# Window attention of a two-block transformer kernel: the constant of the hidden keys written by VectorE, two jobs moved to GpSimd, weights of a gate split earlier

## The reference, cut to what matters

```python
h = rmsnorm_2(x, norm_g)                     # 512 x 1024
q, k, v, za, u, vs, zs, gm = split(h @ w_in) # q 16 heads of 64; k, v 2 heads; za, u, vs, zs 1024 wide
# keys of the own chunk of 64 tokens and of the two chunks before it
s = einsum('bnqhgd,bnkhd->bhgnqk', qc, kb) * 64 ** -0.5
s = where(valid, s, -1e30)
m = maximum(max(s), sink)                    # one sink value for each head
p = exp(s - m)
o = (p / (sum(p) + exp(sink - m))) @ vb
a   = (o * silu(za)) @ w_att_out
sgo = (chunked_spatial_gating(...) * silu(zs)) @ w_sg_out
```

## Time and profile before

| | us |
|---|---|
| median of 3 runs | 1279.54 (1279.12 to 1280.45) |
| profiled execution, own time | 1279.79 |
| its span in the profile | 1278.0 |
| TensorE busy | 1261.3 (99%) |
| VectorE busy | 729.8 (57%) |
| ScalarE busy | 548.2 (43%) |
| GpSimd busy | 84.2 (7%) |
| window attention, from the first mask product to the last gating's input | 859.2 to 959.5 |

### The profile page before, as it was taken

The page is one execution under the profiler, slowest core; times in us unless marked ns, Lnnn a source line. Parts: engine busy times, 40 slices in busy tenths (PEclk is TensorE's granted clock), DMA queues, the critical chain, the costliest instruction groups (busy, mean ns, idle before and its releaser), DMA issues.

```text
span 1278.0 us, 15814 instructions
## 1 busy us (share of the span) xinstructions
PE 1261.3 (99%) x6114; PEld 1058.4 (83%) x6114; DVE 729.8 (57%) x1185; ACT 548.2 (43%) x953; POOL 84.2 (7%) x129
## 2 busy tenths in 40 slices
PE   9999999999999999999999999999999999999997
PEld 8878888888888888888888888878888888888886
DVE  6885677753635444444443349858985436436554
ACT  5456565642334434343322233338763343223233
POOL 0002250220000000000000000002220000000000
PEclk9999999999999999999999999999999999999999
DMA  6241323133532232333323323331104322323221
GB/s 199 68 116 53 83 75 91 51 85 96 181 99 77 89 107 90 99 98 115 99 83 100 115 66 116 99 99 34 50 19 157 118 84 87 102 96 99 84 98 66
DMA packets 106956, 119.54 MB, mean 94 GB/s; under 512 B 13895, under 2 KB 89741, under 8 KB 106893
## 3 DMA queue, kind: packets, MB, share of 16 engines
q1 hardware_dynamic: 106876, 118.67, 29.5%
q10 hardware_dynamic: 16, 0.00, 0.0%
HBM read 113.42 MB, written 2.10 MB: 90 GB/s over the span
## 4 chain that ended last, share of the span: by engine, by line
PE 90%; DVE 6%; ACT 3%; issue 1%; POOL 0%; ACTq 0%; DVEq 0%; POOLq 0%
PE ps_mm L2013 56%; PE ps_mm L2048 23%; PE ps_s L2191 1%; DVE w_lo L1216 1%; PE ps_o L2222 1%; PE ps_o L2440 1%; ACT w_hi L685 1%; PE ps_mm L2105 1%; PE ps_s L2244 1%; PE ps_t L2202 1%; PE ps_t L2427 1%; DVE w_lo L1225 1%; DVE small L1816 1%; PE ps_o L2271 1%; DVE pt_lo L1836 1%
## 5 line engine op out<-in xcount | busy, mean ns | idle before, releaser
L2013 PE MATMUL ps_mm<-act_hi,w_hi 128*128 128x512 f32 x944 | 372.4, 394 | 2.8 <-DVE w_lo L1216 2.8
L2013 PE MATMUL ps_mm<-act_hi,w_lo 128*128 128x512 f32 x944 | 369.9, 392 | 0.0
L2013 PE MATMUL ps_mm<-act_lo,w_hi 128*128 128x512 f32 x944 | 369.8, 392 | 0.0
L1216 DVE TENSOR_TENSOR w_lo<-stage,w_hi 128x2048 fp32r<-128x2048 f32 (+5 forms) x78 | 158.4, 2031 | 160.7 <-ACT w_hi L685 160.5
L2013 PEld LDWEIGHTS ps_mm<-act_hi,w_hi 128*128 128x128 f32 x944 | 177.4, 188 | 39.2 <-DVE w_lo L1216 4.5
L2013 PEld LDWEIGHTS ps_mm<-act_hi,w_lo 128*128 128x128 f32 x944 | 177.4, 188 | 35.5
L2013 PEld LDWEIGHTS ps_mm<-act_lo,w_hi 128*128 128x128 f32 x944 | 177.5, 188 | 34.7
L685 ACT ACTIVATE w_hi<-stage 128x2048 fp32r<-128x2048 f32 (+5 forms) x79 | 133.7, 1693 | 159.9 <-PE ps_mm L2048 112.7
L1622 DVE TENSOR_TENSOR w_lo<-stage,w_hi 128x2048 fp32r<-128x2048 f32 x23 | 52.7, 2292 | 56.3 <-ACT w_hi L965 56.2
L2048 PE MATMUL ps_mm<-w_hi,act_hi 128*128 128x512 f32 (+2 forms) x208 | 77.6, 373 | 0.6 <-DVE lat L1352 0.5
L2048 PE MATMUL ps_mm<-w_lo,act_hi 128*128 128x512 f32 (+2 forms) x208 | 77.1, 370 | 0.0
(11 more groups left out here) (401 smaller groups left out, 2031.9 us busy)
## 6 DMA issues: line engine op xcount, KB each, us to landing
stage<-in_w_in SPq DMA_DIRECT2D x43, 1024.0 KB, 5.3
stage<-in_w_ffn_gate SPq DMA_DIRECT2D x11, 1024.0 KB, 5.3
stage<-in_w_ffn_up SPq DMA_DIRECT2D x11, 1024.0 KB, 5.3
stage<-in_w_ffn_down SPq DMA_DIRECT2D x10, 1024.0 KB, 5.0
stage<-in_w_out SPq DMA_DIRECT2D x4, 1024.0 KB, 5.7
stage<-in_w_att_out SPq DMA_DIRECT2D x4, 1024.0 KB, 5.2
stage<-in_w_sg_out SPq DMA_DIRECT2D x4, 1024.0 KB, 5.5
stage<-in_w_o SPq DMA_DIRECT2D x4, 1024.0 KB, 5.1
```

The costliest lines, as they stand in the source:

```text
L1216: V.tensor_tensor(w_lo[:, s, 0:k * w], stage[:, s, 0:k * w], w_hi[:, s, 0:k * w].bitcast(F32), ALU.subtract).then_inc(w_lo_made, 1)
L2013: ins = T.matmul(ps_mm[:, 2 * bank_slot + m, :], wt[:, kk, m * P:(m + 1) * P], acts[ap][:, kk, :], start=(r == 0), stop=(r == per - 1), sk ...
```

## The change

1. The mask product of each of the 32 pieces goes. The first score product starts the bank, and VectorE writes -1e30 into the corners of `ps_s` by memset, ahead of the maximum: one memset of 64 partitions x 128 elements for pieces 0 to 7, two for the others, and the maximum waits for the last one.
2. GpSimd computes `dsink` (32 times, 128x2) and the gating of zs (8 times), the latter in two instructions of 128x512 with a wait between them, in place of one on VectorE.
3. In the za loop, ScalarE and VectorE split unit za+i+2 at index i (i below 3), ahead of the Silu and behind the two `normed`; the low parts of the keys and of v come later (v's at i = 1), and the row block of `res` comes behind the two `normed`.

```diff
@@ block.gpsimd
-            for q in range(WIN_PIECES):
-                j0, c = 0 if q // 8 else P, 2 * (q % 4)
-                pool.wait_ge(rden_made, q + 1)
-                G.tensor_scalar(prob2[:, q % 4, 256 + j0:512], ...).then_inc(win_p_ready, 1)
+            pool.wait_ge(sink_landed, 16)
+            for p in range(WIN_STEPS + 2):
+                if p < WIN_PIECES:
+                    h, c = window_head(p % 8, 0), 2 * (p % 4)
+                    j = 16 * (p // 8 % 2) + h
+                    pool.wait_ge(win_max_made, p + 1)
+                    G.tensor_tensor(dsink[:, c:c + 2], sinkb[:, h:h + 3:2], nm2[:, j:j + 3:2], ALU.add
+                                    ).then_inc(sink_diff, 1)
+                if 1 <= p <= WIN_PIECES:
+                    q = p - 1
+                    j0, c = 0 if q // 8 else P, 2 * (q % 4)
+                    pool.wait_ge(rden_made, q + 1)
+                    G.tensor_scalar(prob2[:, q % 4, 256 + j0:512], ...).then_inc(win_p_ready, 1)
+                for u, m in WIN_STREAM.banks.get(p - 1, ()):
+                    n = 2 * (u - U0["zs"]) + m
+                    pool.wait_ge(z_tanh, n + 1)
+                    linked_after(G.tensor_scalar(tmp[:, m, :], tmp[:, m, :], 1.0, None, ALU.add))
+                    G.tensor_tensor(gu[:, n, :], tmp[:, m, :], gu[:, n, :], ALU.mult).then_inc(z_gated, 1)
@@ block.scalar
-                if i:
-                    hi(u + 1)
+                if i < 3:
+                    hi(u + 2)
@@ block.vector, the za loop
             for i in range(4):
                 u = U0["za"] + i
-                if i:
-                    lo(u + 1)
-                else:
+                if i == 0:
                     dve.wait_ge(v_turned, 1)
                     ... v2_hi
-                    ... v2_lo, k_lo
-                V.scalar_tensor_tensor(out=res[:, i, :], ...).then_inc(x3_made, 1)
                 for m in range(2):
                     normed(gz[:, 2 * i + m, :], u, m)
+                if i < 3:
+                    lo(u + 2)
+                if i == 0:
+                    ... k_lo
+                if i == 1:
+                    ... v2_lo
+                V.scalar_tensor_tensor(out=res[:, i, :], ...).then_inc(x3_made, 1)
                 if i == 3:
                     dve.wait_ge(x3_made, TT)
@@ block.vector, the window loop
                     dve.wait_ge(win_s_full, p + 1)
+                    sc = ps_s[:, p % 2, :].rearrange("p (e n) -> p e n", e=2)
+                    outside = link(V.memset(sc[0:CHUNK, :, 2 * P - CHUNK:2 * P], NEG))
+                    if b:
+                        outside = link(V.memset(sc[CHUNK:P, :, 0:CHUNK], NEG))
+                    after(outside)
                     after(link(V.tensor_reduce(mx, ps_s[...], AX.X, ALU.max, negate=True)))
                     V.tensor_tensor(nm2[:, j:j + 3:2], mx, nsinkb[:, h:h + 3:2], ALU.min).then_inc(win_max_made, 1)
-                    dve.wait_ge(win_max_made, p + 1)
-                    V.tensor_tensor(dsink[:, c:c + 2], ...).then_inc(sink_diff, 1)
...
-                for u, m in WIN_STREAM.banks.get(p - 1, ()):
-                    z_bank(m, 2 * (u - U0["zs"]) + m)
@@ block.tensor, the window loop
-                    ends = slice(0, 4, 3) if b else slice(3, 4)
-                    T.matmul(ps_s[...][:, :, ends, :], ident_r[:, :], window_r[...][:, :, ends, :],
-                             start=True, stop=False, skip_group_check=True)
                     for e in range(2):
                         T.matmul(out, q_split[...], k_hi[...],
-                                 start=False, stop=False, skip_group_check=True)
+                                 start=True, stop=False)
                         ins = T.matmul(out, q_split[...], k_lo[...],
-                                       start=False, stop=(e == 1), skip_group_check=True)
+                                       start=False, stop=True)
```

More of the change, by code:

```diff
@@ L659, in _ @@
                         pool.wait_ge(diff_rstd_made, hd + 1)
-            for q in range(WIN_PIECES):
-                j0, c = 0 if q // 8 else P, 2 * (q % 4)
-                pool.wait_ge(rden_made, q + 1)
-                G.tensor_scalar(prob2[:, q % 4, 256 + j0:512], prob2[:, q % 4, 256 + j0:512], rden2[:, c + 1:c + 2],
-                                None, ALU.mult).then_inc(win_p_ready, 1)
+            pool.wait_ge(sink_landed, 16)
[10 more added lines that the diff above has]
+                    pool.wait_ge(rden_made, q + 1)
+                    G.tensor_scalar(prob2[:, q % 4, 256 + j0:512], prob2[:, q % 4, 256 + j0:512], rden2[:, c + 1:c + 2],
+                                    None, ALU.mult).then_inc(win_p_ready, 1)
+                for u, m in WIN_STREAM.banks.get(p - 1, ()):
[3 more added lines that the diff above has]
+                    G.tensor_tensor(gu[:, n, :], tmp[:, m, :], gu[:, n, :], ALU.mult).then_inc(z_gated, 1)
         @block.scalar
@@ L1750, in _, with turned_values @@
             normed(kv[:, 0, :], u, 1)
[L1752 to L1756, removed]
+            def turned_values():
+                return ps_t[:, :].rearrange("p (t g n) -> p t g n", t=TT, g=AG)
+            halves = (slice(0, AD), slice(AD, 2 * AD))
             for i in range(4):
                 u = U0["za"] + i
-                if i:
-                    lo(u + 1)
-                else:
+                if i == 0:
                     dve.wait_ge(v_turned, 1)
[L1765 to L1771, removed]
+                    for half in halves:
+                        V.tensor_copy(v2_hi[:, :, :, half], turned_values()).then_inc(v2_wg_made, 1)
+                for m in range(2):
+                    normed(gz[:, 2 * i + m, :], u, m)
+                if i < 3:
+                    lo(u + 2)
+                if i == 0:
                     for g in range(AG):
@@ L1777, in _ @@
                                             ).then_inc(k_lo_made, 1)
+                if i == 1:
+                    for n, half in enumerate(halves):
+                        dve.wait_ge(v2_wg_made, n + 1)
+                        V.tensor_tensor(v2_lo[:, :, :, half], turned_values(), v2_hi[:, :, :, half].bitcast(F32),
+                                        ALU.subtract).then_inc(v2_wg_made, 1)
                 V.scalar_tensor_tensor(out=res[:, i, :], in0=res[:, i, :], scalar=rstd[:, i:i + 1], in1=gf_b[:, :],
                                        op0=ALU.mult, op1=ALU.mult).then_inc(x3_made, 1)
-                for m in range(2):
-                    normed(gz[:, 2 * i + m, :], u, m)
                 if i == 3:
@@ L1819, in _ @@
                     V.tensor_tensor(nm2[:, j:j + 3:2], mx, nsinkb[:, h:h + 3:2], ALU.min).then_inc(win_max_made, 1)
-                    c = 2 * (p % 4)
-                    dve.wait_ge(win_max_made, p + 1)
-                    V.tensor_tensor(dsink[:, c:c + 2], sinkb[:, h:h + 3:2], nm2[:, j:j + 3:2], ALU.add
-                                    ).then_inc(sink_diff, 1)
                 if 1 <= p <= NP:
@@ L2400, in _ @@
                     k0 = (b - 1) * P if b else 0
-                    ends = slice(0, 4, 3) if b else slice(3, 4)
-                    T.matmul(ps_s[:, p % 2, :].rearrange("p (e c n) -> p e c n", e=2, c=4)[:, :, ends, :],
-                             ident_r[:, :], window_r[:, :, :].rearrange("p e (c n) -> p e c n", c=4)[:, :, ends, :],
-                             start=True, stop=False, skip_group_check=True)
                     for e in range(2):
```

## The result

The changed kernel takes 1287.7 us (median of 4 runs, 1286.0 to 1288.0) against 1279.65 us before: ratio 1.0061, 95% interval 1.0048 to 1.0073. It is 8.1 us slower. I had forecast 1281.5 us, in a range from 1276.0 to 1287.0: the direction was right, the size was a quarter of the measured one, and the time lies 0.7 us outside the range. The profiled execution took 1287.59 us, its span is 1285.8 us, 7.8 us more than before.

The account below looks back on a forecast made before the run. TensorE was taken as busy 99% of the span, with VectorE near its limit in the attention. Terms +0.6 (VectorE), +1.6 and +0.3 (GpSimd), -0.5 (za) gave +2.0 us: 1281.5 us, range 1276.0 to 1287.0.

Parts of the forecast that it names:

- The 3.4 us of TensorE: Mask product in the window attention: removing it takes 3.4 us off TensorE, the most this can give.
- the za part: Za loop: the 1.7 us wait goes, 1.2 us is given back at the attention's door, so -0.5 us.
- the stretches with their reserve: Attention, by stretch: VectorE's additions are absorbed up to reserves of 0.6, 1.6 and 1.4 us; sum +0.6 us.
- both inside the reserve: Stretch 898.4 to 916.5: VectorE +0.6, TensorE -0.7, reserve 1.6, so -0.5 us with 0.2 left for uneven steps.
- Part 2: VectorE in an attention step: dsink and gatings leave, memsets come, +0.30 us in 24 steps; by stretches +0.6 us.
- Part 3: GpSimd in the attention: gatings make dsink late, 1.6 us, and shared SBUF reads cost VectorE 0.3 us.
- The memset's term: VectorE's memsets of 64x128 ahead of the maximum: 0.22 us each, 0.50 for two with waits, bounds 0.16 and 0.29 each.
- GpSimd's term: Six gatings on GpSimd: 1.6 us for late dsink (bounds 0.5 and 3.1), 0.3 for SBUF meetings (0 and 1.2).
- The rival's price: Attention: GpSimd stops VectorE's two-operand SBUF instructions until it ends, 6.5 us more, 1288 us; chance 0.12.
- TensorE waiting at the transposes for VectorE's low part, over 2 us in all: Expected sign in the attention's changed profile that VectorE's reserve is gone: over 2 us of such TensorE waits.
- Dear memsets: VectorE's attention steps: memsets cost 0.29 us each, +5.4 us in all, 1284.9 us; chance 0.08.
- TensorE stays the bound: Attention: two memsets cost under about 0.25 us, the 3.4 us come through, 1275.6 us; chance 0.18.

Follow-up runs that it names:

- run 4: The changed kernel with the gating of zs back on VectorE, dsink still on GpSimd: 1285.2 us, ratio 1.0045.
- run 1: The kernel before with only the new za loop (weights split sooner, row block of res behind the two normed): 1278.9 us, ratio 0.9995.
- run 3: The kernel before with only dsink and the gating of zs moved to GpSimd: 1279.6 us, ratio 1.0001.
- run 11: The kernel before with the new za loop, but the last row block of res ahead of the normed: 1277.9 us, ratio 0.9985.
- run 6: The changed kernel without the memsets, so without the mask: 1278.3 us, ratio 0.9991.
- run 8: The changed kernel with GpSimd's gating in four instructions of 256 columns in place of two of 512: 1286.1 us, ratio 1.0052.
- run 5: The changed kernel with dsink back on VectorE, the gating of zs still on GpSimd: 1290.1 us, ratio 1.0085.
- run 7: The changed kernel with the second memset on the first 64 partitions, so a wrong corner is masked: 1283.3 us, ratio 1.0031.
- run 9: The changed kernel with the two corner memsets in turned order in odd pieces, all corners masked: 1285.6 us, ratio 1.0049.
- run 10: The changed kernel with the last row block of res ahead of the two normed of unit za+3: 1285.6 us.

## Why the prediction was right or wrong

- **"VectorE is near its limit, what leaves TensorE is worth something only as far as VectorE follows"** held. The 3.4 us of TensorE bought next to nothing: without the memsets the kernel gains 1.2 us, of which the za part alone gives 0.7, with them it loses 8.1.
- **The step that failed: the stretches with their reserve.** I let VectorE's additions be absorbed up to a reserve, took the gatings' slots off on top, and so came to "both inside the reserve" and a gain for TensorE's two stretches. Beside the forecast of Part 2 and the lateness of Part 3 stands what the maxima say, from the first piece of a line to the last (us; run 4 has no gating on GpSimd):

| pieces | Part 2 | Part 3 | changed kernel | run 4 |
|---|---|---|---|---|
| 0 to 8 | -0.3 | 0.2 | +1.5, with 0.75 of clock | +0.7 |
| 8 to 15 | +0.7 | 1.0 | +2.0 | +1.75 |
| 15 to 21 | -0.5 | 0.3 | +1.8 | +0.9 |
| 21 to 23 | +0.6 | 0 | +1.3 | +1.3 |
| 23 to 30 | -0.3 | 0.45 | +0.9 | +1.0 |
| 30 to 31 | +0.4 | 0 | +0.55 | +0.4 |

The forecast missed most from 15 to 21, by 2.0 us, the first of TensorE's stretches, where both stops fall, and from 8 to 15 by 0.3 only.

- **The size of the two terms.** Without the gatings' slots my Part 2 is 0.4 + 1.5 + 0.2 + 0.6 + 0.7 + 0.4 = +3.8 us; run 4 against run 1, which differ in the mask and `dsink` alone, is +6.2. The gating's place was then worth 0.6 - 3.8 + 1.6 + 0.3 = -1.3 us to me; it measured +1.2 over pieces 10 to 31. Both terms were 2.5 us too low. The remaining 1.4 us of run 4's distance to the changed kernel, the scatter at the first maximum and the clock, were in no term.
- **The memset's term** was mis-sized. I took 0.22 us for the instruction and 0.50 for two with their waits; the row is 0.165, but with the pauses at the change of partitions the pair puts the maximum 0.52 us later behind the gating (0.09 + 0.46 - 0.03) and 0.63 behind other instructions (0.09 + 0.46 + the 0.08 of overlap lost). With 0.20 for `dsink` that is about +0.37 a step in place of +0.30. Run 4's loss from piece 10 to 31 is 5.3 us, and 21 x 0.37 is 7.8; that the 2.5 between them are VectorE's reserve is what is left over, not a measurement. The 0.03 of a result's wait I had counted, the held start I hadn't.
- **GpSimd's term:** 1.6 + 0.3 us forecast, 5.0 gross against 3.9 won. ScalarE waited 1.59, 0.43, 0.97 and 0.44 us where I had 1.7, 1.0, 1.3 and 0.95; the two of 0.4 did not show. The lateness was rather too high, and still the loss was larger, because I let ScalarE's pauses and the longer steps swallow most of it, and because the stops of VectorE that I gave 0.12 as a rival came true in two of six gatings, 1.06 us each, beside a third of 0.15. The Trainium skill, "SBUF — State Buffer", section "Who interferes with whom", says that a VectorE instruction with two SBUF inputs contends with a GpSimd one that reads SBUF, over ports that it calls an exclusive lock; its words "for the whole instruction", which I took for this case, stand there beside VectorE's two-port modes. The row at 905.68 agrees: stopped until GpSimd's product ends. In run 3 a minimum that began 0.21 us into the product took 1.10 us, up to its end as well. But a minimum at 876.88, begun 0.32 us into GpSimd's 1.50 us of adding 1, was over after 0.31 us, so here only the product with two inputs stopped VectorE to its end. The rows that made me doubt it were of GpSimd's scaling, which has one. The other four gatings cost no such stop, since no minimum or sum began during their products. The rival's price (6.5 us more) was too high for that reason. The last gating, which I had at no cost, did stop the full weight split at 971.20 (3.27 us in place of 2.29), but the kernel is 7.7 us behind at the maximum of piece 31 and 7.8 at its end.
- **The za part** was right: -0.5 forecast, -0.7 in run 1, with 1.0 us given back at the door by the medians (run 1 against run 11; 0.3 by their profiled executions), where I had 1.2.
- **What the profile would show.** "TensorE waiting at the transposes for VectorE's low part, over 2 us in all" was no sign of anything: the kernel before has 2.0 us of it, which the earlier trace rows did not show.
- **The rivals.** "Dear memsets" had 0.64 us for the pair, as far over the measured 0.52 to 0.63 as I was under it, and not for the reason that was found; "TensorE stays the bound" had the point from which it decides at 0.25 us for the pair, against 0.5 to 0.6 measured.
- **The end of the sum.** Run 1's -0.7 (za), +6.2 (mask and `dsink`), +1.2 (the gating's place) and 1.4 of scatter and clock are 8.1 us of 8.1. The last two come from single profiles, the others from medians.

## What to carry to other kernels

Where two engines run at 95% side by side, cost an edit on the one that gets work, in starts from one instruction to the next and not in the row's length, and take no credit on the other. A small instruction on GpSimd that others wait for must not be queued behind a long one there, and a long one with two inputs can stop VectorE's small ones with two SBUF inputs until it ends. When a wait is removed by moving work behind something, look at what starts next: the 1.2 us of an unrelated row block took 1.0 us of the 1.7 that the earlier split had won. And before a difference of 1 or 2 us between two runs is put down to an edit, look where in the profile it arises: here 1.2 of it stood ahead of the first instruction that differed.

## What was not expected of the hardware

In three of the profiles TensorE's clock fell at the door. In the changed kernel TensorE did nothing from about 860.7 to 862.5, and then (windows, columns as in the earlier trace rows)

```profile
860.50:862.50 2.00, 0.21 (x1) 0.00 (x0) 1.71 (x8) 0.82 (x5) 0.20 (x1) 0.99 0.00 0
862.50:866.00 3.50, 3.46 (x10) 2.95 (x11) 1.32 (x7) 3.50 (x15) 1.61 (x4) 0.52 0.00 0
866.00:878.60 12.60, 11.70 (x74) 10.10 (x73) 10.78 (x36) 8.63 (x35) 5.12 (x10) 1.00 0.26 84
```

the granted clock is 0.52 for 3.5 us, near the lower level of 1.2 GHz, with 0.43 us from one matmul of 512 columns to the next in place of 0.23. Runs 6 and 8 show the same (0.57), runs 1, 4, 5, 7 and 9 don't, although their wait for the exponential is 1.3 to 1.8 us as well; what decides it stays open. Its cost can be read from kernels with the same instructions up to there: the changed kernel lags behind runs 4, 7 and 9 by 0.62, 0.50 and 0.43 us at the first maximum and by 1.37, 1.25 and 1.19 at the fifth, and behind run 10 by 1.49 and 2.25. That is 0.75 us each time, and it stays. Against run 8, which has the fall too, next to nothing moves: the changed kernel is 0.39 us ahead at the first maximum and 0.45 at the fifth. Whoever compares the profile of the changed kernel with that of a kernel that kept the full clock has to take these 0.75 us off. How often it comes is not known for the executions without a profile: in run 6 the three with a mean clock of 0.998 took 1279.2 to 1279.6 us and the seven with 0.999 took 1277.8 to 1278.8, in run 8 the one with 0.997 took 1287.8 and the others 1285.8 to 1286.3, but the changed kernel's four, 1286.0 to 1288.0 us, do not sort so.

The stop works the other way round too. In run 8 a GpSimd instruction with one input that started 0.01 us behind a long VectorE one with two took 2.99 us, where it takes 0.85 alone (first VectorE, then GpSimd):

```profile
971.77 2.29 DVE L1237 TENSOR_TENSOR w_lo<-stage,w_hi 128x2048 fp32r<-128x2048 f32 x1 [2.50 <-ACT w_hi L706]
971.78 2.99 POOL L682 TENSOR_SCALAR tmp<-tmp 128x256 f32<-128x256 f32 x1
```

And under GpSimd's instruction with one input the changed kernel's minimum is not held to the end (first GpSimd, then VectorE):

```profile
876.56 1.50 POOL L680 TENSOR_SCALAR tmp<-tmp 128x512 f32<-128x512 f32 x1
876.88 0.31 DVE L1839 TENSOR_TENSOR small<-small 128x2 f32<-128x2 f32 x1
```

That the same memset is 0.12 us dearer to follow when it changes partitions (0.26 against 0.14 us from start to start), and that its row shows none of it, was the other surprise.
